# A mixing block's work put in another order, and half of a modulation GEMV summed on VectorE

## What is computed

```python
mod = c_act @ w_ada[l] + b_ada[l]
shift1, scale1, gate1, shift2, scale2, gate2 = jnp.split(mod, 6, axis=-1)
h = modulate(rms_norm(x, norm_mix[l]), shift1, scale1)
(g_q, g_k, g_v, g_z, g_a, g_b, s_q, s_k, s_v) = jnp.split(h @ w_in[l], split_points, axis=-1)
gdn_out = gated_deltanet(g_q, g_k, g_v, g_z, g_a, g_b, conv_w[l], ...)
swa_out = sliding_window_attention(s_q, s_k, s_v, q_norm[l], k_norm[l], sinks[l], positions)
x = x + gate1[:, None, :] * (jnp.concatenate([gdn_out, swa_out], axis=-1) @ w_out[l])
...
out = out + combine[:, e:e + 1] * (hid @ w_down[e])      # 32 experts, two for each token
```

## Time and profile before

| | us |
|---|---|
| median of 3 runs | 2826.25 (2822.76 to 2828.98) |
| the profiled execution | 2825.9 |
| its span, first to last instruction | 2824.1 |
| TensorE matmul busy | 2444.0 (87%) |
| VectorE busy | 880.0 (31%) |
| ScalarE busy | 613.0 (22%) |
| GpSimd busy | 563.8 (20%) |

### The profile page before, as it was taken

The page is one execution under the profiler, slowest core; times in us unless marked ns, Lnnn a source line. Parts: engine busy times, 40 slices in busy tenths (PEclk is TensorE's granted clock), DMA queues, the critical chain, the costliest instruction groups (busy, mean ns, idle before and its releaser), DMA issues.

```text
span 2824.1 us, 30509 instructions
## 1 busy us (share of the span) xinstructions
PE 2444.0 (87%) x12317; PEld 1887.2 (67%) x12318; DVE 880.0 (31%) x1282; ACT 613.0 (22%) x945; POOL 563.8 (20%) x182
## 2 busy tenths in 40 slices
PE   7994857986765999998799997799999977699997
PEld 5453436884533999994588785688875853588785
DVE  4314235432242011012422202333452941423302
ACT  1102322331101000011222212233333311222211
POOL 0000002220010000000434431433431410344331
PEclk8997978998778999999899998899999989899999
DMA  8220410000201788870122222222332222123221
GB/s 261 75 71 19 161 48 1 1 1 0 92 0 45 257 301 289 298 235 3 57 92 89 90 90 82 76 75 83 116 109 82 90 73 69 45 89 97 96 90 67
DMA packets 219925, 276.41 MB, mean 98 GB/s; under 512 B 9655, under 2 KB 199059, under 8 KB 219828
## 3 DMA queue, kind: packets, MB, share of 16 engines
q1 hardware_dynamic: 211744, 267.49, 28.8%
q0 software_dynamic: 1376, 4.26, 0.5%
q10 hardware_dynamic: 6708, 3.29, 0.4%
HBM read 270.79 MB, written 4.24 MB: 97 GB/s over the span
## 4 chain that ended last, share of the span: by engine, by line
PE 81%; DVE 9%; DVEq 3%; ACT 3%; issue 2%; DMA 1%; ACTq 1%; POOL 0%; SPq 0%; POOLq 0%
PE bank L2084 38%; PE bank L1761 8%; PE bank L1769 4%; PE bank L592 3%; PE bank L431 2%; PE bank L1559 2%; PE bank L575 2%; PE bank L2850 2%; PE bank L1971 2%; PE bank L1453 2%; PE bank L1243 1%; PE bank L2732 1%; PE bank L1236 1%; DVE arena L2819 1%; PE bank L2751 1%
## 5 line engine op out<-in xcount | busy, mean ns | idle before, releaser
L2084 PE MATMUL bank<-hT_high_split,ring_split 128*128 128x512 f32 x2496 | 797.2, 399 | 64.1 <-DVEq L2160 45.8
L2084 PEld LDWEIGHTS bank<-hT_high_split,ring_split 128*128 128x128 f32 x2496 | 472.1, 189 | 174.1 <-DVEq L2160 46.3
L2068 POOL TENSOR_TENSOR ring_split<-ring,ring_split 128x2048 fp32r<-128x2048 f32 x66 | 306.3, 4643 | 1080.5 <-ACT ring_split L2063 1080.5
L2084 PE MATMUL bank<-hT_split,ring_split 128*128 128x512 f32 x1248 | 491.9, 394 | 0.0
L2063 ACT ACTIVATE ring_split<-ring 128x2048 fp32r<-128x2048 f32 x104 | 198.9, 1915 | 700.5 <-DMA ring<-in_ffn_w_up 227.1
L2084 PEld LDWEIGHTS bank<-hT_split,ring_split 128*128 128x128 f32 x1248 | 236.4, 189 | 57.4 <-issue 0.2
L2308 POOL TENSOR_TENSOR ring_split<-ring,ring_split 128x2048 fp32r<-128x2048 f32 x38 | 176.2, 4639 | 373.0 <-ACT ring_split L2063 373.0
L1761 PE MATMUL bank<-arena,ring 128*128 x2048 | 235.3, 276 | 5.2 <-issue 5.2
L1761 PEld LDWEIGHTS bank<-arena,ring 128*128 128x128 f32 x2048 | 232.6, 193 | 5.4 <-issue 5.4
L2084 PE MATMUL bank<-ring_split,hid_high_split 128*128 128x512 f32 x704 | 225.4, 402 | 7.4 <-DVE hid_low_split L2170 7.4
L2084 PEld LDWEIGHTS bank<-ring_split,hid_high_split 128*128 128x128 f32 x704 | 134.5, 191 | 41.1 <-DVE hid_low_split L2170 8.2
(11 more groups left out here) (410 smaller groups left out, 2806.4 us busy)
## 6 DMA issues: line engine op xcount, KB each, us to landing
...
```

The source lines that it names most:

```text
L2068: pool.tensor_tensor(low(n), raw(n), high(n).bitcast(F32), ALU.subtract)\
L2084: mm = pe.matmul(dst, left[l], right[r], start=start and n == 0, stop=stop and n == 2)
```

## The change

- The ring's order and `pe_proj1` begin with `sq` and `skv`; the gate columns follow `sq`, then come the 12 convolved blocks. z is made last, after the transposes of `pe_qkv` (`pe_z`), and `pe_swa_turn` waits for its copies.
- `dve_swa_prep` is taken apart. Angles come before the convolutions, the sums behind block 0, the reciprocal behind block 2, the rotation of tile t behind block 6 + t. The 16 multiplications by the norm's factors go to GpSimd (`pool_swa_prep`). ScalarE's root, sines and exponential follow its blocks 2, 3 and 4.
- The gates of the delta net are made behind blocks 1 and 5, their sums on TensorE behind block 11. The rest of `dve_gdn_prep` stands before the attention. Of its 28 scalings 12 stay on VectorE, 16 go to GpSimd with the two memsets (`pool_gdn_prep`). The barrier before the attention is gone, and GpSimd's with it.
- Of the 16 slots of `ada2` TensorE makes the even ones only. VectorE sums each odd one over two units, four instructions in each (`dve_ada2_part`). The turning of row or sum into columns is done within the next unit, two matmuls each, instead of 32 at the end; slots are given back two at a time.
- `dve_more_list` moves ahead of the copies of the gathering; the overflow expert's gate and up weights no longer wait for the gathering's end, only its down weight does.
- The positions are loaded before the ring's first slots. The arena grows from 29900 to 30096 columns.

```diff
+        plan("sq", n_slots(w_in, 2064, 2064 + 512))
+        plan("skv", t_slots(w_in, 2576, 2832))
         plan("qkv", t_slots(w_in, 0, QKV))
         plan("z", n_slots(w_in, QKV, QKV + 512))
-        plan("sq", n_slots(w_in, 2064, 2064 + 512))
-        plan("skv", t_slots(w_in, 2576, 2832))
...
         def pe_ada2(pe, u):
-            if u >= 1:
+            pe_ada2_turn(pe, u - 1)
+            if u % 2 == 0:
+                s = FIRST["ada2"] + u
+                need(pe, s)
+                w = slot_view(s, 256)
+                for k in range(KD):
+                    mm = pe.matmul(bank[7][0:1, 0:256], cact[:, k:k + 1], w[:, k, :], start=(k == 0),
+                                   stop=(k == KD - 1))
+                mm.then_inc(S("ada_ps"), 1)
+        def act_ada2(act, u):
+            if u % 2 == 0:
+                nxt(act, "ada_ps")
+                act.activation(ada_row[0:1, :], bank[7][0:1, 0:256], ACT.Copy).then_inc(S("ada_taken"), 1)
+        def pe_ada2_turn(pe, u):
+            if u < 0:
+                return
+            if u % 2 == 0:
                 nxt(pe, "ada_taken")
-            s = FIRST["ada2"] + u
-            need(pe, s)
+            else:
+                nxt(pe, "ada_acc")
+            for j in range(2):
+                c = slice(P * j, P * j + P)
+                left, right = (ada_row[0:1, c], one[0:1, :]) if u % 2 == 0 else (ada_sum[:, u // 2 % 2, c], one)
+                mm = pe.matmul(bank[7][:, 256 + 2 * u + j:257 + 2 * u + j], left, right, start=True, stop=True)
+            if u % 2 == 1:
+                mm.then_inc(S("slots_used"), 2)
+            if u == 15:
+                pe.drain().then_inc(S("ada_turned"), 1)
+        def dve_ada2_part(dve, u):
+            i = u // 2
+            s = FIRST["ada2"] + 2 * i + 1
             w = slot_view(s, 256)
-        def act_ada2(act, u):
-            act.wait_ge(S("slots_used"), FIRST["ada2"] + u + 1)
-            act.activation(ada_row[0:1, 256 * u:256 * u + 256], bank[7][0:1, 0:256], ACT.Copy)\
-               .then_inc(S("ada_taken"), 1)
-        def pe_ada2_turn(pe):
-            nxt(pe, "ada_taken")
-            for m in range(32):
-                mm = pe.matmul(bank[7][:, 16 + m:17 + m], ada_row[0:1, P * m:P * m + P], one[0:1, :],
-                               start=True, stop=True)
-            mm.then_inc(S("ada_turned"), 1)
+            acc = ada_sum[:, i % 2, :]
+            if u % 2 == 0:
+                dve.wait_ge(loaded[s % RING], 16 * (s // RING + 1))
+                if i >= 2:
+                    dve.wait_ge(S("slots_used"), FIRST["ada2"] + 2 * i - 2)
+                dve.tensor_scalar(acc, w[:, 0, :], cact[:, 0:1], None, ALU.mult)
+            for k in range(1, 4) if u % 2 == 0 else range(4, KD):
+                dve.drain()
+                mm = dve.scalar_tensor_tensor(acc, w[:, k, :], cact[:, k:k + 1], acc, ALU.mult, ALU.add)
+            if u % 2 == 1:
+                mm.then_inc(S("ada_acc"), 1)
...
         def pe_proj1(pe):
-            nxt(pe, "conv_in", 2)
+            pe_gemm_n(pe, FIRST["sq"], tokens, bank[2:6])
-            nxt(pe, "z_taken")
             nxt(pe, "sq_taken")
+            pe_gdn_sums(pe)
+            nxt(pe, "conv_in", 2)
+        def pe_z(pe):
+            nxt(pe, "skv_taken")
+            pe_gemm_n(pe, FIRST["z"], tokens, bank[2:6])
...
+            act.activation(g_ea, row("a_log").unsqueeze(1).broadcast_to([P, NT, H]), ACT.Exp)
+            nxt(act, "proj1_done")
+            act.activation(g_beta, b_in, ACT.Sigmoid).then_inc(S("g_beta"), 1)
+            nxt(act, "skv_taken")
+            act.activation(squares_q, sq, ACT.Square)
+            act.activation(squares_k, sk3, ACT.Square).then_inc(S("w_squares"), 1)
...
+                if m == 2:
+                    nxt(act, "w_ss")
+                    act.activation(w_r, w_ss, ACT.Sqrt, bias=eps, scale=1.0 / HD).then_inc(S("w_roots"), 1)
+                if m == 3:
+                    nxt(act, "angles")
+                    act.activation(sin, ang, ACT.Sin)
+                    act.activation(cos, turns, ACT.Sin).then_inc(S("rotation"), 1)
+                if m == 4:
+                    nxt(act, "g_abs")
+                    act.activation(g_e, g_s, ACT.Exp, scale=-1.0).then_inc(S("g_exp"), 1)
...
         def dve_proj1(dve):
             dve.memset(convin[:, :, 0:3], 0.0)
+            dve.wait_ge(S("slots_used"), FIRST["sq"] + 2)
+            for t in range(NT):
+                i = dve.tensor_copy(sq[:, t, :], bank[2 + t][:, :])
+            i.then_inc(S("sq_taken"), 1)
+            nxt(dve, "ab_ps")
+            dve.tensor_copy(ab, bank[6][:, 0:64].rearrange("p (t n) -> p t n", n=16)).then_inc(S("proj1_done"), 1)
+            dve_angles(dve)
+            dve.wait_ge(S("slots_used"), FIRST["skv"] + 1)
+            for t in range(NT):
+                i = dve.tensor_copy(skv[:, t, :], bank[2 + t][:, 0:256])
+            i.then_inc(S("skv_taken"), 1)
             for m in range(NM):
+                dve_conv1(dve, m)
+                if m == 0:
+                    dve_swa_sums(dve)
+                if m == 1:
+                    dve_gdn_abs(dve)
+                if m == 2:
+                    nxt(dve, "w_roots")
+                    dve.reciprocal(w_ss, w_r).then_inc(S("w_recip"), 1)
+                if m == 5:
+                    dve_gdn_gate(dve)
+                if m == 6:
+                    nxt(dve, "w_normed")
+                    nxt(dve, "rotation")
+                if 6 <= m < 6 + NT:
+                    dve_rope(dve, m - 6)
+            dve.drain().then_inc(S("w_qk"), 1)
+        def dve_z(dve):
             dve.wait_ge(S("slots_used"), FIRST["z"] + 2)
             for t in range(NT):
                 i = dve.tensor_copy(z[:, t, :], bank[2 + t][:, :])
             i.then_inc(S("z_taken"), 1)
...
+        def pool_swa_prep(pool):
+            nxt(pool, "w_recip")
             for t in range(NT):
                 k4 = sk3[:, t, :].rearrange("p (h e) -> p h e", e=HD)
+                pool.tensor_tensor(sq4[:, t], sq4[:, t], w_ss[:, t, 0:H].unsqueeze(2).broadcast_to([P, H, HD]), ALU.mult)
+                pool.tensor_tensor(k4, k4, w_ss[:, t, H:NW].unsqueeze(2).broadcast_to([P, 2, HD]), ALU.mult)
+            nxt(pool, "rows_loaded", 16 * len(ROWS))
+            pool.drain()
             for t in range(NT):
                 k4 = sk3[:, t, :].rearrange("p (h e) -> p h e", e=HD)
+                pool.tensor_tensor(sq4[:, t], sq4[:, t], row("q_norm").unsqueeze(1).broadcast_to([P, H, HD]), ALU.mult)
+                i = pool.tensor_tensor(k4, k4, row("k_norm").unsqueeze(1).broadcast_to([P, 2, HD]), ALU.mult)
+            i.then_inc(S("w_normed"), 1)
...
         def pe_swa_turn(pe):
             nxt(pe, "w_qk")
+            nxt(pe, "z_taken")
...
-            pe_ada2_turn(pe)
+            pe_ada2_turn(pe, 15)
...
+                dve_ada2_part(dve, u)
...
+            scaled(dve, kn, kn, g_ss[:, :, H:2 * H]).then_inc(S("g_normed"), 1)
+            scaled(dve, qn, qn, g_ss[:, :, 0:H])
+            dve.drain()
             nxt(dve, "g_exps")
+            scaled(dve, qg, qn, g_expG)
             dve.drain().then_inc(S("g_scaled"), 1)
+        def pool_gdn_prep(pool):
+            nxt(pool, "g_beta")
+            nxt(pool, "qkv_taken", 3 * NT)
+            scaled(pool, vb, vb, g_beta)
+            nxt(pool, "g_normed")
+            nxt(pool, "g_exps")
+            scaled(pool, kdec, kn, g_kdec)
+            scaled(pool, kb, kn, g_beta)
+            pool.drain()
+            scaled(pool, kbG, kb, g_expG)
+            pool.memset(state, 0.0)
+            pool.memset(vnew, 0.0)
+            pool.drain().then_inc(S("g_parts"), 1)
...
+            pe.drain().then_inc(S("o_free"), 1)
...
+            dve_more_list(dve)
             for k in range(KD):
                 nxt(dve, "m_x_ps", 2)
...
         def sp_more(sp):
             nxt(sp, "h2_ready", NT)
-            nxt(sp, "m_x_ps", 2 * KD)
             def body(n):
                 ex = sp.value_load(o_expert[0:1, bass.ds(n, 1)], min_val=0, max_val=N_EXP - 1)
                 sp.wait_ge(S("o_free"), n + 1)
                 sp.dma_start(o_gu[:, 0], flat_rows(w_gate, ex, F_EXP)).then_inc(S("o_loaded"), 16)
                 sp.dma_start(o_gu[:, 1], flat_rows(w_up, ex, F_EXP)).then_inc(S("o_loaded"), 16)
+                sp.wait_ge(S("m_x_ps"), 2 * KD)
                 sp.dma_start(o_dn, flat_rows(w_down, ex, D)).then_inc(S("o_loaded"), 16)
...
+            sp_positions(sp)
             load(sp, 0, FIRST["ada2"])
-            sp_positions(sp)
...
             act_qkv(act)
-            meet(act)
-            act_swa_prep(act)
+            act_gdn_prep(act)
             act_swa_turn(act)
             act_swa(act)
             meet(act)
-            act_gdn_prep(act)
...
             pe_qkv(pe)
-            meet(pe)
+            pe_z(pe)
             pe_swa_turn(pe)
             pe_swa(pe)
             meet(pe)
-            pe_gdn_prep(pe)
+            nxt(pe, "g_scaled")
```

(10 more changed lines are left out.)

221 lines of the change are left out of this document (89 added, 132 removed).

## The result

The changed kernel took 2723.2 us (median of 4 runs, 2720.6 to 2725.0), the kernel before 2827.2 (2822.8 to 2829.0) on the same chip: a ratio of 0.9634, 95% interval 0.9617 to 0.965. The forecast of 2729.7 lies 6.5 us above. In the profiled executions the span went from 2824.1 to 2718.7 us, 105.4 less, and the mean granted clock from 0.923 to 0.935.

The account below looks back on a forecast made before the run. It saw VectorE work standing alone between stages where VectorE is three quarters idle, with TensorE waiting; 25.0 + 16.5 + 34.6 + 1 + 18.6 + 0.5 = 96.2 off 2825.9 gave 2729.7 us, range 2710 to 2760 (own range 2720 to 2742).

Parts of the forecast that it names:

- Part 1: Stretch up to the attention: TensorE's reordered stages laid end to end finish at 245.9 instead of 270.9, 25.0 us less.
- a block's cover of 6.8 of 6.9 us: Convolutions: VectorE's convolution plus rotation, 6.8 us, fits beside TensorE's 6.9 per block for four blocks; nothing counted.
- rival 4: Convolutions: VectorE runs late through GpSimd's interference or the rotation; 10 us give 2740; chance 0.05.
- Part 3: Between attention and delta net: 35.9 us shrink to 1.3, 34.6 less, plus 1 for a warmer start.
- a warmer start: Delta net's opening: may give 1 us more (0 to 5), its first stretch having waited through a window at 0.50.
- The two engines' interference: Delta net's preparation beside z: VectorE's 12 scalings waiting for GpSimd's would add 12.6 us; taken as nothing.
- Part 2: Attention with the row's turning: 126.5 us become 110.0, 16.5 less, bounds 99 and 153.
- The walk: Attention units stepped through by engine and semaphore at full clock: 116.8 us before, 94.4 after, four units in 25.1.
- the short pauses: Attention: TensorE's pauses of 1.0 us, whose clock effect no row showed; 4.1 us taken, from 0 to 47.
- Rival 1: Attention: the low clock stays for most of the stage, 130 to 153 us, time 2750 to 2773; chance 0.18.
- Part 4: Overflow expert: TensorE starts at 876.6 instead of 895.19, 18.6 us less (15 to 19), plus 0.5 for a warmer start.
- the reading of registers: Overflow expert: about 1.7 us between the gate matmuls and TensorE's expert start.

Follow-up runs that it names:

- a_reorder: Changed kernel with all GEMV slots back on TensorE and the overflow expert's list and DMAs back in place, leaving the reordering and new turning: 2763.5 us.
- b_gemv: Kernel before with only the GEMV's part of the change (odd slots summed on VectorE, turning within the next unit): 2810.5 us.
- b_expert: Kernel before with only the overflow expert's part of the change (earlier list, gate and up weights loaded at once): 2807.2 us.
- b_late: Kernel before with only the attention's outputs of a token tile moved one unit later on VectorE: 2808.3 us.
- a_prepafter2: Changed kernel with the delta net's preparation alone put back behind the attention: 2743.7 us.
- a_vnorm: Changed kernel with the multiplications given to GpSimd back on VectorE, in the new order: 2725.4 us.
- a_warm2: Changed kernel with 11 matmuls, results unread, put before the turning of units 5, 9 and 13 to fill TensorE's 4.1 us waits: 2717.4 us.
- a_late: Changed kernel with VectorE's attention outputs of a token tile one unit later, behind the accumulation: 2702.7 us.
- a_pegemv_late: Changed kernel with all 16 GEMV slots back on TensorE and the attention's outputs one unit later: 2717.7 us.
- a_late_pre: Changed kernel with the attention's outputs one unit later, but in front of that unit's accumulation on VectorE: 2714.6 us.

## Why the prediction was right

The total was 6.5 us too high. Parts 2 and 4 are each confirmed by a run of their own; parts 1 and 3 only together, by a_reorder (63.9, with some 4 of the new turning in it, against 60.6 forecast), and their division by one profile.

- **Part 1** (25.0 forecast): 26.8. `sq` 29.4 (29.2), the convolutions 82.6 (82.4), the idle time behind them 4.3 (5.0), transposes 9.6 (10.3) and z 27.6 (27.5) came as laid end to end. The term that was too big is `ab`, 8.9 instead of 10.7, at clock 0.78 and not 0.65. That is mostly the execution that was read: unchanged and in the old order, `ab` took 9.1 to 9.2 us in b_gemv, b_expert and b_late. For the same reason the 26.8 is not sharper than some 4 us, as the first scores of the old order came at 270.9 in one execution and at 273.6 to 274.7 in three. That a block's cover of 6.8 of 6.9 us would do was right: TensorE never waited in the convolutions, though VectorE was busy for 53.5 us of them; rival 4 did not occur.
- **Part 3** (34.6 + 1): the 35.9 us fell to 1.4 as said. The 1 for a warmer start did not come; the first 25 us stood at 0.64 as before. The step to sharpen is what this sum stands for: a_prepafter2 shows 29.3 of it to be the place and 5.2 the gates' operations made elsewhere. The second engine is worth nothing where the preparation stands alone (19.9 us from first scaling to TensorE's start, against 19.0), and under 2 us beside z (a_vnorm).
- **The two engines' interference.** 12 scalings on VectorE took 13.24 us where a_vnorm's cost 0.62 each, 5.8 more. I had taken nothing, with 12.6 as the upper bound; it was about half, and the time left before z's end (4.2 us were still over) hid it. The reason that I gave for nothing, that GpSimd waits for the scaled keys first, held for the first five scalings only. The rule weighed in the prediction, of the Trainium skill (SBUF — State Buffer, Who interferes with whom), has the two exclude each other for an instruction's whole length; by it, each of the seven that overlapped would have waited for one of GpSimd's 1.05 us. The trace comes close: each of the seven took 1.46 us instead of 0.62, so 0.84 more, and the two engines' instructions came one for one, a pair in 1.46 us where one after the other they are 1.67.
- **Part 2** (16.5): 20.9 in the attention by the profiles, 17 to 18 by the two runs that take or give this part alone. The walk foresaw cycles of 25.1 at full clock and of 28.5 with a restart; they took 27.4, with the pause 4.11 instead of 4.4. a_warm2's cycle at full clock took 24.4, so the walk was 0.7 too long and a restart cost 3.0, not 3.4. For the short pauses I had 4.1, and there the three GEMVs of the first units, behind pauses of 1.0 to 2.5 us, took 1.2, 1.7 and 1.3 us more than at full clock; the later pauses of 0.85 cost nothing (3.61 at 324.27). Rival 1, that the clock stays low for most of the stage, did not occur: 0.79, and full level in between the restarts, so a pause of 4.11 us brought the clock down for some 10 us here and no longer.
- **Part 4** (18.6 + 0.5): 20.0 and 1.6. Ready earlier, the expert started 0.28 us behind the gate's last matmul; I had put 1.7 us for the reading of registers there, of which the trace shows nothing on the way. The 1.6 are the expert's first matmuls (64 records), 7.41 us instead of the 9.01 that they took at first half, then full clock behind 20.32 us of idleness.
- **What the prediction did not see** is that the pause it priced so closely could be taken away. It named the wait (output, scaling, exponentials) and treated it as given. By a_late it was worth 16.9 us of stage (20 of time), about as much as the GEMV's split (18.9 of stage, 17 of time), and by a_pegemv_late and a_late together the split is worth 11.6 us once the pause is gone, not 17. The walk made for a_late had the late outputs at 12.3 us at full clock; the rest of the time came from restarts that no longer occur and from the delta net's opening.
- **What stays open:** which course the clock takes in the delta net's opening. 0.64 and 220 us, or 0.93 and more and 214 to 215, occurred (with a_late_pre and a_pegemv_late in between), with no relation to the idle time just before (1.37 us ahead of 0.64 and of 0.94 in the changed kernel and a_warm2; 24.0 ahead of 0.64 and 28.2 ahead of 0.93 in the kernel before and a_prepafter2). Differences of 5 us between kernels here can be this alone, and with one profile for each kernel no run shows whether the course belongs to the kernel or to the execution; it stands in the table so that it can be taken out.
